# Row sums of three norms: one product of plain float32 with ones replaced by two products of rounded parts

## The chip, the cores and the metric

The kernel runs on one core of a Trainium2 chip. The metric is the device time of one execution in microseconds. Three executions of the kernel before took 1333.63 to 1334.12 us, with a median of 1333.63 us.

## The reference

Two transformer blocks in float32, applied one after the other to 512 tokens of width 1024. The first has four mixers (short convolution, stick-breaking attention, a Mamba-2 mixer, block attention), gates, an output projection and a gated feed-forward net of hidden width 2816. The second has sliding-window attention with sinks, spatial gating and an output projection. The change concerns the places where a row's mean square is taken:

```python
def rmsnorm(x, g):
    xf = x.astype(jnp.float32)
    y = xf * lax.rsqrt(jnp.mean(xf * xf, axis=-1, keepdims=True) + RMS_EPS)
    return (y * g.astype(jnp.float32)).astype(x.dtype)
...
    x = x + merged @ w_o
    h2 = rmsnorm(x, norm2_g)                      # norm 1 of the change
    g_ff, up_ff = jnp.split(h2 @ w_gate_up, 2, axis=-1)
    return x + (jax.nn.silu(g_ff) * up_ff) @ w_down
...
    return rmsnorm(h, final_g)[:, :seq]           # norm 2: end of the first block
...
        h = rmsnorm_2(x, norm_g[l])               # norm 3: start of the second block
        proj = h @ w_in[l]
```

## The kernel before

Activations lie with features on the 128 partitions and the 512 tokens along a row: `xT` is eight tiles of 128x512. Every weight matrix is streamed in **units** of 1024 (or fewer) rows by 256 columns; a unit gives two output **tiles** of 128x512, in one of four PSUM banks `G` each. All large products are made in three parts of a rounded type (fp32r): a weight is split into `whi` (rounded, a copy by ScalarE, `split(n)`) and `wlo` (the rest, four subtractions of 128x512 by GpSimd), an activation into `hh` and `hl`. One tile of a unit is `gemm_fm`: eight times `whi` with `hh` and with `hl` (lines 592 and 593), then eight times `wlo` with `hh` (line 600). `unit_last_k` does the same for the first unit behind a norm, but leaves the three products of the last k for both tiles to the end (lines 659 to 661), since that piece of `hh` and `hl` comes last.

Each engine has a program of its own, in an order written out by hand, and they are tied by semaphores. An engine carries out its program in order: behind an instruction that waits, all later ones of its engine wait. `hi_done` counts the finished `whi` (a unit's first product waits for its own), `lo_done` the finished halves of `wlo`, `tile_done` and `tile_free` the PSUM tiles.

A norm is not applied ahead of its product. The weights are multiplied with `x*g`, and the result is scaled with `R`, the reciprocal root of the row's mean square, spread over the partitions. For `R` the squares of the eight tiles are added on VectorE into `acc0` (128x512), and TensorE multiplies that with a 128x128 matrix of ones (`ones`, in the constants `c1`), which sums over the partitions and spreads the sum: line 893. ScalarE takes the root from the bank `M[0]` (lines 1142 and 1143). For the two norms between the blocks there are `acc1` and `acc2` (lines 909 and 910), and `R` is made from both in a longer chain between ScalarE and VectorE. These products are plain float32.

What ScalarE has to do behind these sums, in its order:

```python
            act.wait_ge(sem("norm_ps"), 1)
            rsqrt(R[:, :], M[0][:, :], DM).then_inc(sem("R2"), 1)

            for f, (n0, part, h0) in enumerate(ffn_units):
                with act.Fori(0, part // 2) as i:
                    for j in range(2):
                        n = n0 + j
                        split(n + 1, i)
```

So `whi` of the second feed-forward unit is made behind the wait for the first sum (`norm_ps` 1). Behind the second sums (`norm_ps` 2) stand, in this order, lines 1347, 1348, 1350, 1142 and 1143 (the roots), the wait for `key_s` (VectorE makes it from `R`), four DMA issues of `key_t` (line 1360), and then `split` of the unit `n_qz + 1`.

The names of the units around the two places: `n_c0` to `n_c0 + 3` are the output projection of block one; the feed-forward units begin at `ffn_units[0]` (below "the first feed-forward unit"); `n_e0` is the unit of keys and values of block two, `n_qz` and `n_qz + 1` are the first of its queries and gates. `turn_rows` and `turn_keys` are small transposes (lines 917, 922 and 930) that stand between tiles of `n_qz`; `turn_rows` needs `R` of the second block (semaphore `R3`).

Of the kernel before, what the change touches and what calls it, by code (L numbers as in the profile page):

```python
# [27 lines left out]
SEQ, DM = 512, 1024  # L28
P = 128
KD = DM // P  # L30
# [45 lines left out]
def build_program(nc, x, par, cst1, cst2a, w_in, w_branch, w_o, w_gu, w_down, w_in2, sg_w, sg_b, ln_g,  # L76
                  ln_b, w_ao, w_so, w_o2, out):
    f32, f32r = mybir.dt.float32, mybir.dt.float32r
# [6 lines left out]
    with ctx:  # L85
        base = (nc.sbuf_base + 31) // 32 * 32

        def place(name, shape, kb, dt=f32):

            return nc.alloc_sbuf_tensor_at(name, shape, dt, offset=base + int(kb * KB))  # L90
# [3 lines left out]
        def sem(name):  # L94
            if name not in sems:
                sems[name] = ctx.enter_context(nc.semaphore(name))
            return sems[name]
# [10 lines left out]
        hh = place("hh", [P, KD, SEQ], 76, f32r)  # L108
        hl = place("hl", [P, KD, SEQ], 92, f32r)
        c1 = place("c1", [P, 640], 108)  # L110
        prm = place("prm", [P, NPAR], 112)
        sml = place("sml", [P, 256], 113)
        R = place("R", [P, SEQ], 114)
        Z0 = 116.0
# [42 lines left out]

        acc0 = place("acc0", [P, SEQ], Z0)
        sq0 = place("sq0", [P, 2, SEQ], Z0 + 2)

        ah = place("ah", [P, 8, SEQ], Z0, f32r)
        al = place("al", [P, 8, SEQ], Z0 + 16, f32r)
# [1 line left out]
        fu_t = place("fu_t", [P, 2, SEQ], Z0 + 68)  # L164
        acc1 = place("acc1", [P, SEQ], Z0 + 32)
        acc2 = place("acc2", [P, SEQ], Z0 + 34)
        sq1 = place("sq1", [P, 2, SEQ], Z0 + 36)
        sq2 = place("sq2", [P, 2, SEQ], Z0 + 40)
        r1 = place("r1", [P, SEQ], Z0 + 44)
# [112 lines left out]
        def as_f32(ap):  # L282
            return ap.bitcast(f32)
# [288 lines left out]
        def _(pe):  # L572
# [64 lines left out]
            def unit_last_k(n, xh, xl, kts, ready, between=None, between_at=0):  # L637

                last_k, s = kts - 1, n % 2
                tiles = [(bank_of(tiles_before(n) + j), j * P) for j in range(2)]  # L640
                for j, (bank, col) in enumerate(tiles):
                    pe.wait_ge(sem("tile_free"), free_before(tiles_before(n) + j))
                    if j == 0:
                        pe.wait_ge(sem("hi_done"), n + 1)
                    for k in range(last_k):
                        if j == 0:
                            pe.wait_ge(sem(ready[0]), ready[1] + k + 1)
                        w = whi[:, s, k, col:col + P]
                        mm(bank[:, :], w, xh[:, k, :], start=(k == 0), stop=False)  # L649
                        mm(bank[:, :], w, xl[:, k, :], start=False, stop=False)  # L650
                    pe.wait_ge(sem("lo_done"), 2 * n + 1 + j)
                    for k in range(last_k):
                        mm(bank[:, :], wlo[:, s, k, col:col + P], xh[:, k, :], start=False, stop=False)  # L653
                    if between and j == between_at:
                        between()
                pe.wait_ge(sem(ready[0]), ready[1] + kts)
                for bank, col in tiles:
                    w = whi[:, s, last_k, col:col + P]
                    mm(bank[:, :], w, xh[:, last_k, :], start=False, stop=False)
                    mm(bank[:, :], w, xl[:, last_k, :], start=False, stop=False)  # L660
                    mm(bank[:, :], wlo[:, s, last_k, col:col + P], xh[:, last_k, :], start=False, stop=True).then_inc(sem("tile_done"), 1)
# [227 lines left out]
            for f, (n0, part, h0) in enumerate(ffn_units):  # L889
                if f == 0:  # L890
                    def sum_rows():
                        pe.wait_ge(sem("acc0"), KD)
                        mm(M[0][:, :], ones, acc0[:, :], start=True, stop=True).then_inc(sem("norm_ps"), 1)
                    unit_last_k(n0, hh, hl, KD, ("h_lo", KD), sum_rows)
                    unit_fm(n0 + 1)
                with pe.Fori(1 if f == 0 else 0, part // 2) as i:
                    for s in range(2):
                        n = 2 * i + n0 + s
                        for j in range(2):
                            b = (tiles_before(n0) + 2 * s + j) % 4  # L900
                            gemm_fm((4 * i + tiles_before(n0) + 2 * s + j, b), n, (n0 + s) % 2, hh, hl, KD, j * P, j == 0)
                unit_last_k(n0 + part, ah, al, part, ("act_lo", h0))
                for p in range(1, 4):
                    unit_fm(n0 + part + p, ah, al, part)


            def sum_both():
                pe.wait_ge(sem("acc2"), KD)
                mm(M[0][:, :], ones, acc1[:, :], start=True, stop=True)
                mm(M[1][:, :], ones, acc2[:, :], start=True, stop=True).then_inc(sem("norm_ps"), 1)  # L910
            unit_last_k(n_e0, hh, hl, KD, ("h_lo", 2 * KD), sum_both, 1)

            def turn_rows():

# [81 lines left out]
            for p in range(4):  # L996
                n = n_qz + 2 * p
                for u in range(2):
                    for j in range(2):
                        gemm_fm(tiles_before(n + u) + j, n + u, (n + u) % 2, hh, hl, KD, j * P, j == 0,  # L1000
                                hooks={at: w_slot for at in W_AT[2 * u + j]} if p else None)
                        if p == 0 and u == 0:
                            (turn_rows, turn_keys)[j]()
            for p in range(4):
                n = n_vs + p
                wide_unit(n, p % 2, tiles_before(n - p % 2), lambda t: w_slot())
# [514 lines left out]
        def _(dve):  # L1521
# [4 lines left out]
            def link(ins):  # L1526

                links[0] += 1
                ins.then_inc(sem("dve_link"), 1)
                dve.wait_ge(sem("dve_link"), links[0])  # L1530
# [35 lines left out]

            dve.wait_ge(sem("r_ps"), 1)
            link(v.tensor_copy(R[:, :], M[0][:, :]))
            v.memset(cbuf[:, :, 0:2], 0.0)
            link(v.memset(xbuf[:, :, 0:3], 0.0))  # L1570
            link(v.memset(wdt[:, :, :], 0.0))
# [248 lines left out]
            def accumulate(acc, sq, m, name):  # L1820
                if m == 0:
                    v.tensor_copy(acc[:, :], sq[:, 0, :]).then_inc(sem(name), 1)
                else:
                    dve.wait_ge(sem(name), m)
                    tt(acc[:, :], acc[:, :], sq[:, m % 2, :], ALU.add).then_inc(sem(name), 1)
# [5 lines left out]
            for m in range(KD):  # L1831
                add_residual(tiles_before(n_c0) + m, m)
                dve.wait_ge(sem("h_hi"), KD + m + 1)
                stt(out=hl[:, m, :], in0=xT[:, m, :], scalar=pcol("g2", m), in1=as_f32(hh[:, m, :]),
                    op0=ALU.mult, op1=ALU.subtract).then_inc(sem("h_lo"), 1)
                dve.wait_ge(sem("sq0"), m + 1)
                accumulate(acc0, sq0, m, "acc0")
            dve.wait_ge(sem("R2"), 1)


# [39 lines left out]


            dve.wait_ge(sem("acc1"), KD)
            v.memset(key_t[:, :, :], 0.0)
            link(v.memset(rope_t[:, :, :], 0.0))
            dve.wait_ge(sem("rms12"), 1)
# [321 lines left out]
```

## Time and profile before

| what | value |
|---|---|
| median of three executions | 1333.63 us |
| the profiled execution | 1333.23 us |
| its span, first to last instruction | 1331.2 us |
| TensorE busy | 1321.4 us, 99% of the span |
| VectorE, ScalarE, GpSimd busy | 582.5, 509.6, 597.1 us (44, 38, 45%) |
| mean granted TensorE clock | 0.998 of full speed |
| share of DMA queue q1 of its engines' span | 30.7% |

What lies outside the span is 2.0 us. A row of the timeline gives the start in us, the duration in us, the engine (PE is TensorE, DVE is VectorE, ACT is ScalarE, POOL is GpSimd), the line, the instruction, what it writes and reads, the shape and how many are taken together; in brackets stands how long the engine was idle before and what released it. TensorE's products are pipelined: one of 128x512 is shown as 0.39 us long, while the next starts before it has ended, so the cost of one is the distance of starts. A plain float32 product appears as two records.

### The profile page before, as it was taken

How to read it: one execution, taken by the hardware profiler on the slowest of the kernel's cores; microseconds unless marked ns; L12 is line 12 of the kernel's file. 1: busy time of each engine (PE TensorE's matmuls, PEld its weight loads, DVE VectorE, ACT ScalarE, POOL GpSimd, SP SyncE). 2: the span in 40 equal slices, each digit the busy share in tenths (PEclk: the TensorE clock that was granted, in tenths of full speed). 3: DMA queues.
4: the chain of work that ended last, by engine and by line, in shares of the span. 5: the costliest groups of instructions: out<-in, count | busy, mean ns of one | idle time of the engine just before them, and what ended most of it. 6: DMA issues, size and time to landing. Idle time of an engine off the chain costs nothing.

```text
span 1331.2 us, 16999 instructions
## 1 busy us (share of the span) xinstructions
PE 1321.4 (99%) x6518; PEld 1081.4 (81%) x6518; DVE 582.5 (44%) x947; ACT 509.6 (38%) x729; POOL 597.1 (45%) x448
## 2 busy tenths in 40 slices
PE   9999999999999999999999999999999999999998
PEld 8877777888888888888888887877777888888887
DVE  3674444556554433213322347766654322242333
ACT  6222534566433533222211236254655224342233
POOL 4453333443644364445554546433432553435441
PEclk9999999999999999999999999999999999999999
DMA  6333152413233343333333323322221332423321
GB/s 202 95 113 102 40 151 64 126 41 119 79 97 134 95 115 106 95 95 95 95 95 95 87 71 111 103 69 77 91 68 59 127 95 64 127 64 100 102 83 64
DMA packets 144493, 126.70 MB, mean 95 GB/s; under 512 B 4464, under 2 KB 139760, under 8 KB 144432
## 3 DMA queue, kind: packets, MB, share of 16 engines
q1 hardware_dynamic: 144080, 125.66, 30.7%
q8 instruction: 43, 0.70, 0.2%
q10 hardware_dynamic: 352, 0.19, 0.1%
q14 instruction: 18, 0.15, 0.0%
HBM read 120.46 MB, written 2.10 MB: 92 GB/s over the span
## 4 chain that ended last, share of the span: by engine, by line
PE 96%; DVE 2%; ACT 1%; issue 0%; DMA 0%; SPq 0%; ACTq 0%; DVEq 0%
PE gemm L592 25%; PE gemm L600 25%; PE gemm L593 25%; PE gemm L649 2%; PE gemm L650 2%; PE gemm L653 2%; PE gemm L616 2%; PE gemm L617 2%; PE gemm L622 2%; PE mix L978 1%; PE mix L966 1%; PE mix L955 1%; PE mix L1032 1%; PE mix L802 1%; PE gemm L677 1%; PE mix L827 0%
## 5 line engine op out<-in xcount | busy, mean ns | idle before, releaser
L525 POOL TENSOR_TENSOR wlo<-raw,whi 128x512 fp32r<-128x512 f32 x424 | 571.9, 1379 | 551.0 <-ACT whi L1130 551.0
L592 PE MATMUL gemm<-hh,whi 128*128 128x512 f32 x1128 | 444.9, 394 | 0.4 <-ACT whi L1130 0.4
L593 PE MATMUL gemm<-hl,whi 128*128 128x512 f32 x1128 | 439.6, 390 | 0.0
L600 PE MATMUL gemm<-hh,wlo 128*128 128x512 f32 x1128 | 280.3, 390 | 0.0
L1130 ACT ACTIVATE whi<-raw 128x2048 fp32r<-128x2048 f32 x106 | 202.5, 1911 | 193.4 <-PE gemm L600 164.6
L592 PEld LDWEIGHTS gemm<-hh,whi 128*128 128x128 f32 x1128 | 211.8, 188 | 49.2 <-issue 4.6
L593 PEld LDWEIGHTS gemm<-hl,whi 128*128 128x128 f32 x1128 | 212.0, 188 | 43.1 <-issue 0.5
L600 PEld LDWEIGHTS gemm<-hh,wlo 128*128 128x128 f32 x1128 | 211.4, 188 | 43.6
L521 POOL TENSOR_TENSOR wlo_b<-raw_b,whi_b 128x512 fp32r<-128x512 f32 x16 | 20.6, 1287 | 146.2 <-ACT whi L1130 146.2
L1850 DVE TENSOR_TENSOR fu_t<-gemm,R 128x512 f32<-128x512 f32 x22 | 15.2, 691 | 99.7 <-PE gemm L600 99.7
L592 PE MATMUL gemm<-ah,whi 128*128 128x512 f32 x132 | 51.5, 390 | 0.5 <-DVE xT L1829 0.5
L593 PE MATMUL gemm<-al,whi 128*128 128x512 f32 x132 | 51.4, 389 | 0.0
L1797 DVE TENSOR_TENSOR gt<-gemm,R 128x512 f32<-128x512 f32 x32 | 22.0, 688 | 65.5 <-PE gemm L600 65.4
L1147 ACT ACTIVATE gt<-gt 128x512 f32<-128x512 f32 x32 | 20.1, 627 | 71.7 <-DVE gt L1797 71.7
L1327 ACT ACTIVATE fg_t<-fg_t 128x512 f32<-128x512 f32 x22 | 13.9, 633 | 84.6 <-DVE fg_t L1848 84.6
L1869 DVE TENSOR_TENSOR xT<-xT,gemm 128x512 f32 x16 | 11.0, 687 | 70.0 <-PE gemm L600 57.0
L616 PE MATMUL gemm<-whi,hh 128*128 128x512 f32 x96 | 39.2, 408 | 0.0
L617 PE MATMUL gemm<-whi,hl 128*128 128x512 f32 x96 | 37.6, 391 | 0.0
L1848 DVE TENSOR_TENSOR fg_t<-gemm,R 128x512 f32<-128x512 f32 x22 | 15.2, 691 | 48.1 <-PE gemm L600 39.8
L1857 DVE TENSOR_TENSOR al<-fu_t,ah 128x512 f32 x22 | 34.7, 1576 | 2.7
L600 PE MATMUL gemm<-ah,wlo 128*128 128x512 f32 x132 | 33.0, 390 | 0.0
L1371 ACT ACTIVATE wp<-mix,sml 128x256 f32<-128x256 f32 (+1 forms) x64 | 27.7, 452 | 10.5 <-DVE sml L1947 10.5
(443 smaller groups left out, 1863.9 us busy)
## 6 DMA issues: line engine op xcount, KB each, us to landing
raw<-w_in SPq DMA_DIRECT2D x53, 1024.0 KB, 5.3
raw<-w_gu SPq DMA_DIRECT2D x44, 512.0 KB, 4.7
raw<-w_o SPq DMA_DIRECT2D x8, 1024.0 KB, 5.1
raw<-w_down SPq DMA_DIRECT2D x16, 512.0 KB, 4.0
raw_b<-w_branch SPq DMA_DIRECT2D x16, 256.0 KB, 5.6
raw<-w_ao SPq DMA_DIRECT2D x4, 1024.0 KB, 5.1
raw<-w_so SPq DMA_DIRECT2D x4, 1024.0 KB, 5.0
raw<-w_in SPq DMA_DIRECT2D x7, 512.0 KB, 4.6
```

The source lines that it names most:

```text
L525: last = nc.gpsimd.tensor_tensor(a(wlo), a(raw), as_f32(a(whi)), ALU.subtract)
L592: mm(bank[:, :], w, xh[:, k, :], start=(k == 0), stop=False)
L593: mm(bank[:, :], w, xl[:, k, :], start=False, stop=False)
L600: last = mm(bank[:, :], wlo_[:, s, k, col:col + P], xh[:, k, :], start=False, stop=(k == kts - 1))
L616: mm(o, hh[:, 4 * half + i, tok], w, start=(half == 0 and i == 0), stop=False)
L617: mm(o, hl[:, 4 * half + i, tok], w, start=False, stop=False)
L622: last = mm(o, hh[:, 4 * half + i, tok], w, start=False, stop=(half == 1 and i == 3))
L649: mm(bank[:, :], w, xh[:, k, :], start=(k == 0), stop=False)
L650: mm(bank[:, :], w, xl[:, k, :], start=False, stop=False)
L1130: fn(a(whi), a(raw), ACT.Copy).then_inc(sem("hi_done"), 1)
L1371: last = fn(wp[:, s % 3, h, w_from(s):], w_score[:, h, e, w_from(s):], ACT.Exp, bias=w_min(v)[:, h, e:e + 1], accum_out=w_sums(v)[:, h, e, ...
L1857: tt(flat(al), fu_t[:, s, :], as_f32(flat(ah)), ALU.subtract).then_inc(sem("act_lo"), 1)
```

## The change

For each of the three sums VectorE splits the accumulated squares into a rounded part (`acc0h`, `acch`) and a rest (`acc0l`, `accl`), both in the rounded type, and TensorE multiplies each with a rounded matrix of ones (`ones_r`, copied once at the start) and adds the two in PSUM. The first sum moves from behind the first tile of its unit to behind the second. The two later sums move out of unit `n_e0` into the first tile of `n_qz`, behind its tenth product; `turn_rows` moves from between the tiles of `n_qz` to behind the tenth product of the second tile.

```diff
@@ [buffers]
+        ones_r = place("ones_r", [P, P], 110.5, f32r)
...
+        acc0h = place("acc0h", [P, SEQ], Z0 + 6, f32r)
+        acc0l = place("acc0l", [P, SEQ], Z0 + 8, f32r)
...
+        acch = place("acch", [P, 2, SEQ], Z0 + 48, f32r)
+        accl = place("accl", [P, 2, SEQ], Z0 + 52, f32r)
@@ [TensorE]
                     def sum_rows():
-                        pe.wait_ge(sem("acc0"), KD)
-                        mm(M[0][:, :], ones, acc0[:, :], start=True, stop=True).then_inc(sem("norm_ps"), 1)
-                    unit_last_k(n0, hh, hl, KD, ("h_lo", KD), sum_rows)
+                        pe.wait_ge(sem("ones_r"), 1)
+                        pe.wait_ge(sem("acc0_lo"), 2)
+                        mm(M[0][:, :], ones_r[:, :], acc0h[:, :], start=True, stop=False)
+                        mm(M[0][:, :], ones_r[:, :], acc0l[:, :], start=False, stop=True).then_inc(sem("norm_ps"), 1)
+                    unit_last_k(n0, hh, hl, KD, ("h_lo", KD), sum_rows, 1)
...
             def sum_both():
-                pe.wait_ge(sem("acc2"), KD)
-                mm(M[0][:, :], ones, acc1[:, :], start=True, stop=True)
-                mm(M[1][:, :], ones, acc2[:, :], start=True, stop=True).then_inc(sem("norm_ps"), 1)
-            unit_last_k(n_e0, hh, hl, KD, ("h_lo", 2 * KD), sum_both, 1)
+                pe.wait_ge(sem("acc_lo"), 3)
+                for i in range(2):
+                    mm(M[i][:, :], ones_r[:, :], acch[:, i, :], start=True, stop=False)
+                    last = mm(M[i][:, :], ones_r[:, :], accl[:, i, :], start=False, stop=True)
+                last.then_inc(sem("norm_ps"), 1)
+            unit_last_k(n_e0, hh, hl, KD, ("h_lo", 2 * KD))
...
                         gemm_fm(tiles_before(n + u) + j, n + u, (n + u) % 2, hh, hl, KD, j * P, j == 0,
-                                hooks={at: w_slot for at in W_AT[2 * u + j]} if p else None)
-                        if p == 0 and u == 0:
-                            (turn_rows, turn_keys)[j]()
+                                hooks={at: w_slot for at in W_AT[2 * u + j]} if p else {10: (sum_both, turn_rows)[j]} if u == 0 else None)
+                        if p == 0 and u == 0 and j == 1:
+                            turn_keys()
@@ [VectorE]
             link(v.tensor_copy(R[:, :], M[0][:, :]))
+            dve.wait_ge(sem("c1_in"), 16)
+            v.tensor_copy(ones_r[:, :], ones).then_inc(sem("ones_r"), 1)
...
                 accumulate(acc0, sq0, m, "acc0")
+            dve.wait_ge(sem("acc0"), KD)
+            v.tensor_copy(acc0h[:, :], acc0[:, :]).then_inc(sem("acc0_lo"), 1)
+            dve.wait_ge(sem("acc0_lo"), 1)
+            tt(acc0l[:, :], acc0[:, :], as_f32(acc0h[:, :]), ALU.subtract).then_inc(sem("acc0_lo"), 1)
             dve.wait_ge(sem("R2"), 1)
...
             dve.wait_ge(sem("acc1"), KD)
+            v.tensor_copy(acch[:, 0, :], acc1[:, :])
+            dve.wait_ge(sem("acc2"), KD)
+            v.tensor_copy(acch[:, 1, :], acc2[:, :]).then_inc(sem("acc_lo"), 1)
+            dve.wait_ge(sem("acc_lo"), 1)
+            for i, a in enumerate((acc1, acc2)):
+                tt(accl[:, i, :], a[:, :], as_f32(acch[:, i, :]), ALU.subtract).then_inc(sem("acc_lo"), 1)
             v.memset(key_t[:, :, :], 0.0)
```

ScalarE's and GpSimd's programs have the same instructions in the same order as before. What moves is shown for TensorE at the two places. (`mix` is a bank of `M`, `gemm` one of `G`, `c_58` holds `ones` and the identity.)

**The first feed-forward unit.** Before, the sum stands between its two tiles:

```order
L653 MATMUL gemm<-hh,wlo 128x512 [waits lo_done]
L653 MATMUL gemm<-hh,wlo 128x512 x6
L893 MATMUL mix<-acc_103,c_58 128x512 [waits acc0]
L649 MATMUL gemm<-hh,whi 128x512 [waits tile_free]
L650 MATMUL gemm<-hl,whi 128x512
```

Now the second tile's 21 products come first, then the two products of the sum, the six of the last k, and the first of the next unit:

```order
L658 MATMUL gemm<-hh,wlo 128x512 [waits lo_done]
L658 MATMUL gemm<-hh,wlo 128x512 x6
L899 MATMUL mix<-acc0h,ones_r 128x512 [waits acc0_lo,ones_r]
L900 MATMUL mix<-acc0l,ones_r 128x512
L664 MATMUL gemm<-hh,whi 128x512 [waits h_lo]
...
L597 MATMUL gemm<-hh,whi 128x512 [waits hi_done,tile_free]
```

The sum moved behind 21 products; behind its own two products only six more lie ahead of the next unit's wait for `hi_done`.

**Between the blocks.** Before, the two sums stand ahead of the last six products of `n_e0`:

```order
L653 MATMUL gemm<-hh,wlo 128x512 x6
L909 MATMUL mix<-acc_109,c_58 128x512 [waits acc2]
L910 MATMUL mix<-acc_110,c_58 128x512
L659 MATMUL gemm<-hh,whi 128x512 [waits h_lo]
...
L592 MATMUL gemm<-hh,whi 128x512 [waits hi_done,tile_free]
```

Now they stand in the first tile of `n_qz`, and `turn_rows` (lines 926 and 931) in the second:

```order
L597 MATMUL gemm<-hh,whi 128x512 [waits hi_done,tile_free]
...
L917 MATMUL mix<-acch,ones_r 128x512 [waits acc_lo]
L918 MATMUL mix<-accl,ones_r 128x512
L917 MATMUL mix<-acch,ones_r 128x512
L918 MATMUL mix<-accl,ones_r 128x512
...
L926 MATMUL mix<-c_58,R 128x128 [waits R3]
L926 MATMUL mix<-c_58,R 128x128 x3
L931 MATMUL mix<-c_58,sgw 128x128 [waits sgw_in]
L931 MATMUL mix<-c_58,sgw 128x128 x7
```

The sums moved behind 16 products (six of `n_e0`, ten of `n_qz`).

ScalarE's rows behind the second sums are the same in both kernels but for line numbers; here they are of the changed one:

```order
L1356 ACTIVATE r_118<-mix,prm 128x512 [waits norm_ps]
L1357 ACTIVATE r_119<-r_118 128x512 [waits act_link]
L1359 ACTIVATE r_118<-r_118 128x512 [waits rms12]
L1151 ACTIVATE r_119<-r_119,prm 128x512 [waits n3_var]
L1152 ACTIVATE r_119<-r_119 128x512 [waits act_link]
L1363 ACT_TABLE_LOAD
L1369 DMA key_t<-key_s 8x512 [waits key_s]
L1369 DMA key_t<-key_s 8x512 x3
L1139 ACTIVATE whi<-raw 128x2048 [waits tile_done,raw_in0]
```

The last row is the split of `n_qz + 1`; nothing moved here.

## Rows read from the trace of the kernel before

**Rows 1.** Clock of the core, and the chain that ended last, by engine

```profile
core 0: 1331.2 us, clock 0.998
PE 96%; DVE 2%; ACT 1%; issue 0%; DMA 0%; SPq 0%; ACTq 0%; DVEq 0%
```

**Rows 2.** Timeline, TensorE, first feed-forward unit and the start of the next

```profile
459.05 1.02 PE L893 MATMUL mix<-acc,c 128*128 128x512 f32 x2
...
464.72 0.39 PE L659 MATMUL gemm<-hh,whi 128*128 128x512 f32 x1
...
466.08 0.39 PE L592 MATMUL gemm<-hh,whi 128*128 128x512 f32 x1
```

**Rows 3.** Timeline, ScalarE, same stretch

```profile
460.11 0.69 ACT L1142 ACTIVATE R<-mix,prm 128x512 f32<-128x512 f32 x1 [2.35 <-PE mix L893]
...
462.77 1.92 ACT L1130 ACTIVATE whi<-raw 128x2048 fp32r<-128x2048 f32 x1
```

**Rows 4.** Timeline, VectorE and GpSimd, same stretch

```profile
456.64 0.68 DVE L1825 TENSOR_TENSOR acc<-acc,sq 128x512 f32<-128x512 f32 x1
...
464.77 11.13 POOL L525 TENSOR_TENSOR wlo<-raw,whi 128x512 fp32r<-128x512 f32 x8 [11.81 <-ACT whi L1130]
```

**Rows 5.** Timeline, TensorE, units n_e0, n_qz, first product of n_qz + 1

```profile
825.90 1.02 PE L909 MATMUL mix<-acc,c 128*128 128x512 f32 x2
...
827.84 0.40 PE L660 MATMUL gemm<-hl,whi 128*128 128x512 f32 x1
...
829.00 0.40 PE L592 MATMUL gemm<-hh,whi 128*128 128x512 f32 x1
...
834.47 0.60 PE L917 MATMUL mix<-c,R 128*128 128x128 f32 x4
...
835.69 0.47 PE L592 MATMUL gemm<-hh,whi 128*128 128x512 f32 x1
...
841.62 0.48 PE L592 MATMUL gemm<-hh,whi 128*128 128x512 f32 x1
```

**Rows 6.** Timeline, ScalarE, behind the second sums (ACTq: DMA issues)

```profile
827.81 0.69 ACT L1347 ACTIVATE r<-mix,prm 128x512 f32<-128x512 f32 x1 [0.71 <-PE mix L910]
...
834.29 3.70 ACTq L1360 DMA_DIRECT2D key_t<-key_s  x4
838.10 1.92 ACT L1130 ACTIVATE whi<-raw 128x2048 fp32r<-128x2048 f32 x1 [5.42 <-issue]
```

**Rows 7.** Timeline, VectorE and GpSimd, around the second sums

```profile
824.02 1.29 DVE L1825 TENSOR_TENSOR acc<-acc,sq 128x512 f32<-128x512 f32 x2 [0.38 <-ACT sq L1342]
...
831.41 0.69 DVE L1888 TENSOR_TENSOR R<-r,r 128x512 f32<-128x512 f32 x1 [1.46 <-ACT r L1143]
...
825.87 5.01 POOL L525 TENSOR_TENSOR wlo<-raw,whi 128x512 fp32r<-128x512 f32 x4 [3.22 <-ACT whi L1130]
```

**Rows 8.** Timeline, VectorE and GpSimd, copies and subtractions beside each other

```profile
489.70 0.43 DVE L1855 TENSOR_SCALAR ah<-fu_t 128x512 f32 x1
490.25 1.62 DVE L1857 TENSOR_TENSOR al<-fu_t,ah 128x512 f32 x1
...
490.03 5.49 POOL L525 TENSOR_TENSOR wlo<-raw,whi 128x512 fp32r<-128x512 f32 x4 [5.09 <-ACT whi L1130]
...
468.03 1.28 DVE L1855 TENSOR_SCALAR ah<-fu_t 128x512 f32 x1 [0.16 <-DVE fu_t L1853]
...
818.23 3.27 DVE L1825 TENSOR_TENSOR acc<-acc,sq 128x512 f32<-128x512 f32 x2
```

**Rows 9.** Timeline, TensorE, a short wait for whi

```profile
1027.83 0.50 PE L592 MATMUL gemm<-hh,whi 128*128 128x512 f32 x1 [0.42 <-ACT whi L1130]
```

**Rows 10.** Timeline, TensorE, start of the program

```profile
1.06 4.21 PE L677 MATMUL gemm<-warm 128*128 128x128 f32 x18 [1.06 <-DVE warm L1554]
...
6.21 2.62 PE L677 MATMUL gemm<-warm 128*128 128x128 f32 x22
```

## The prediction

> **What bounds the kernel now.** I read the chain that ended last first: 96% of it is TensorE, at a mean granted clock of 0.998, its upper level of 2.4 GHz [rows 1]. So TensorE's own work and its pauses are the time, and whatever else lies beside it costs nothing until TensorE waits for it. Then I read the timeline of TensorE at the three sums, for what a product costs and where the next wait for another engine stands; then ScalarE's timeline at the same places, for what is queued behind the sum; then VectorE and GpSimd.
>
> A product of the rounded type costs 0.227 us: the six of the last k run from 464.72 to 466.08 [rows 2]. Below that is a slot. Two plain float32 sums cost 827.84 - 825.90 less one slot, 1.71 us, so 0.86 each [rows 5].
>
> **What the change takes away.** Three products of 0.86 become six slots. 2.57 - 1.36 = 1.2 us less for TensorE: 0.4 at the first place, 0.8 at the second. That is 0.09% of the time, under half of the 0.2% that a measurement of this kernel can tell from no change.
>
> **What VectorE gets.** One copy of 128x128 at the start, far smaller than the 128x512 copy beside which I price it: at most the 0.43 us of `ah` [rows 8]. VectorE goes into the next tiles with TensorE tens of slots away from needing them, and the constants it waits for have already served the transposes that released it. I count nothing, at worst 0.4 for the queue behind it on VectorE, which TensorE would not feel. Then three casts and three subtractions of 128x512. No cast from float32 to the rounded type stands on VectorE before. The nearest row is `ah`, one input, one output of the same shape: 0.43 us, or 1.28 with GpSimd busy [rows 8]. The subtraction is like `al`.
>
> At the first place this is free. The last addition ends at 456.64 + 0.68 = 457.32 [rows 4]. Cast and subtraction, 1.28 + 1.62 at their worst, are done by 460.3 with handovers, and GpSimd sleeps until 464.77 [rows 4], so rather by 458.7. TensorE comes for them at 463.8 (below).
>
> **First place, the sum that comes later.** This decides. The sum is not on ScalarE's way by accident: behind its wait stand the two root instructions, a table load, and `whi` of the next unit, and TensorE starts that unit with a wait for this `whi`. Before, ScalarE starts at 460.11, which is 0.04 after the sum's last record ends (459.05 + 1.02 = 460.07), and `whi` runs from 462.77 to 464.69 [rows 2, 3]. TensorE starts the unit at 466.08 [rows 2]. So there are 1.4 us to spare.
>
> After: the second tile starts at 459.05, where the sum stood. 21 slots take 4.76, so the sum starts at 463.81, its second product at 464.04, and that record ends 0.39 later, at 464.43. ScalarE starts at 464.47, 4.36 later than before. Nothing behind it gets shorter, so `whi` runs from 467.13 to 469.05. TensorE ends the sum at 464.27 and the six last products at 465.63, and waits 3.4 us. The handover takes 0.08 or less (`whi` ends at 464.69, GpSimd starts at 464.77 [rows 3, 4]); the first product after such a pause is 0.50 long, not 0.39 [rows 9], 0.11 more. TensorE is where it was at 466.08 at about 469.2. **Place one: +3.1 us**, the gain of 0.4 already in it.
>
> Is something else late next? GpSimd needs 1.39 a subtraction (11.13 for eight [rows 4]); the first half of `wlo` is there 2.9 after `whi`, at 472.0. TensorE wants it after 16 slots, at 472.8. It holds, with 0.8 to spare. The unit after that has the whole 10.9 us of a unit for its `whi`.
>
> **Second place.** Without the sums the six last products run from 825.90 to 827.26, and `n_qz` starts there instead of at 829.00. Its `whi` is ready, since GpSimd began on it at 825.87 [rows 5, 7]. Ten slots later, at 829.53, TensorE wants the four split tiles.
>
> VectorE's last addition ends at 824.02 + 1.29 = 825.31 [rows 7]. Two casts of 0.43 bring it to 826.1 or 826.2. From 825.87 GpSimd works beside it. A subtraction that met GpSimd just after it had begun ended 1.84 after GpSimd's start (490.25 + 1.62 - 490.03 [rows 8]). Two such one behind the other, from 826.0 on, end at 829.7. TensorE waits 0.2 for them and starts the sums at 829.73. The lower end: two additions beside GpSimd took 3.27 together [rows 8], so 829.45, no wait. The upper end: one cast also meets GpSimd and takes 1.28, which moves everything by 0.85 to 1.0: a wait of 1.2. I take 0.2, as the single row describes this case, a start right behind GpSimd's.
>
> On this the Trainium skill, "SBUF — State Buffer", section "Who interferes with whom", says that one pair of ports serves both engines, that a VectorE instruction with two SBUF inputs collides with a GpSimd one that reads SBUF, and that who comes second is blocked for the other's whole instruction. By that rule each subtraction waits out one of GpSimd's 1.25 us (5.01 / 4) and then takes 0.69, and the two end at 829.9; by the row of the two additions it is 829.45. The sum would be larger by 0.2 or smaller by 0.2.
>
> Now ScalarE. Before it starts at 827.81 [rows 6], again 0.04 behind the last record (827.18 + 0.59). After: the fourth product starts at 829.73 + 0.68, ends at 830.80, ScalarE starts at 830.84: 3.03 later. The whole chain behind it hangs together: roots, `R` at 831.41 on VectorE [rows 7], `key_s`, four DMA issues from 834.29 for 3.70, then `whi` of `n_qz + 1` from 838.10 to 840.02 [rows 6]. All of it moves by 3.03, so that `whi` is ready at 843.05. Before, TensorE needed it at 841.62 [rows 5], 1.6 after it was ready.
>
> What does TensorE do until then? From 829.73 four slots and 14 slots end the first tile at 833.8. Ten slots more bring it to `turn_rows` at 836.1. That needs `R`, 832.10 + 3.03 = 835.13: no wait. The transposes take 1.22 (834.47 to 835.69 [rows 5]), 14 slots end the tile at 840.5, `turn_keys` takes under 0.4. TensorE stands at `n_qz + 1` at 840.9 and starts at 843.1, a wait of 2.2. Against 841.62: **place two: +1.5 us**. The slow first product was there before too (0.48 [rows 5]), so no extra for it. The queries' DMAs on SP and GpSimd's subtractions, which hang on the same chain, come 3.0 later as well, but the units behind need them some 10 us on.
>
> **Sum.** 3.1 + 1.5 = +4.6 us on the profiled execution's 1333.23, so 1337.8. The median shown is 0.4 above that execution, so I predict 1338.2, 0.34% slower. Should ends be taken at their lower bounds it is 1337.4, with the late casts 1339.3: that is the main case's own range.
>
> **Rivals.**
>
> *The clock falls in the first pause.* For it: 3.4 us without a product is three times the longest wait that TensorE has anywhere now, the 1.06 at the start [rows 10]. The first 18 records of the program took 4.21 us, 0.234 each, the next 22 only 0.119 each [rows 10], which is what 1.2 and 2.4 GHz would give. A second start like that loses 4.21 - 18 x 0.119 = 2.1 us: 1340.3. Against it: the array worked without a gap up to the pause, and before the start it had not worked at all. The Trainium skill, "TensorE: Matmul & The Clock Gate", section "HAM oscillation — how this bites in real kernels", says that a long enough pause puts the array back to half clock and that the next work then begins cold; no trace here shows a pause of this length. Chance 0.13.
>
> *The casts are slow or collide.* One more microsecond at place two, 1339.2. For it: the one 1.28 in rows 8; against: the casts come before GpSimd starts. Chance 0.14.
>
> *The pauses at place two are swallowed.* If the chain behind the second sums is shorter than it seems, or its DMA issues were waiting for something that doesn't move, only the gain of 0.8 is left there: 3.1 - 0.8, 1335.9, within 0.2% of now. Against it: the rows join without a gap. Chance 0.07. If place one is swallowed instead: -0.4 + 1.5, 1334.7. Chance 0.04.
>
> *No wait at all: not slower.* If the `whi` at 462.77 belonged to a unit that TensorE needs one unit later, there would be 10.9 us more to spare, both delays would vanish, and what stays is the 1.2 of the products: 1332.4, no measurable change. It decides at a delay of 1.4 us at place one (I have 4.36) and 1.6 at place two (3.03). Against it: the order of ScalarE's program names the unit, and GpSimd begins 0.08 after it. Chance 0.08.
>
> *A later wait grows from these.* `wlo` late at place one by more than its 0.8 to spare, or the attention's first steps: 1341 or more. Chance 0.04.
>
> **The numbers.** The main case has 0.50. Slower by over 0.2% (above 1336.3): 0.50 + 0.13 + 0.14 + 0.04 = 0.81. Within 0.2%: 0.07 + 0.04 + 0.06 of the 0.08. Faster by over 0.2% needs 2.7 us where all the sums together cost 2.6: only the remaining 0.02. The range reaches down to the case of one swallowed place and up to the fallen clock: 1335.8 to 1340.4.
>
> **What would show it.** The sums: six records of 0.39 a slot apart, none of 0.59. First place: ScalarE's root 4.4 after where it was in relation to the unit's start, `whi` 4.4 later, and a wait of TensorE for `whi` of 3.4 us, by far the longest of the run. Second place: a wait of 0 to 0.3 at the sums for VectorE, one of about 2 at `n_qz + 1` for `whi`. If the granted clock dips after the first wait, the second rival holds. If TensorE shows no wait for `whi` at either place, I have read ScalarE's order wrongly, and the time will be under the one before.

## The result, and the profile after

The changed kernel takes 1339.99 us, the median of six executions (1338.94 to 1340.73). Six of the kernel before beside it took 1333.60 us (1333.50 to 1334.12). The ratio is 1.0046, with an interval of 1.0036 to 1.0057: slower by 6.4 us, where 4.6 were forecast.

The profiled execution took 1339.9 us, 6.67 more than the one of before. Its span and clock, the chain that ended last, and TensorE's waits:

```profile
core 0: 1337.8 us, clock 0.997
```

```profile
PE 95%; DVE 2%; ACT 2%; DMA 1%; issue 0%; ACTq 0%; SPq 0%; DVEq 0%
```

```profile
PE gemm L597 <- ACT whi L1139: 5.5, 3, 3.4
PE gemm L682 <- DVE warm L1563: 1.1, 1, 1.1
...
PE mix L674 <- DMA xtm<-x: 0.6, 1, 0.6
```

The first row has grown: 5.5 us in three waits for a `whi`, the longest of them 3.4, where the kernel before has one such wait, of 0.4 us. The chain is still TensorE's, so what counts is where its timeline is longer than before. First the first feed-forward unit, which answers to [rows 2]:

```profile
464.37 0.39 PE L899 MATMUL mix<-acc0h,ones_r 128*128 128x512 f32 x1
464.60 0.39 PE L900 MATMUL mix<-acc0l,ones_r 128*128 128x512 f32 x1
...
465.96 0.39 PE L666 MATMUL gemm<-hh,wlo 128*128 128x512 f32 x1
469.75 0.77 PE L597 MATMUL gemm<-hh,whi 128*128 128x512 f32 x1 [3.40 <-ACT whi L1139]
470.31 0.63 PE L598 MATMUL gemm<-hl,whi 128*128 128x512 f32 x1
```

The two products of the sum stand one slot apart and cost a slot each. Then come the six of the last k, and then 3.40 us of nothing. ScalarE's rows say what it was doing, as in [rows 3]:

```profile
465.03 0.69 ACT L1151 ACTIVATE R<-mix,prm 128x512 f32<-128x512 f32 x1 [6.70 <-PE mix L900]
...
467.69 1.91 ACT L1139 ACTIVATE whi<-raw 128x2048 fp32r<-128x2048 f32 x1
```

It stood idle for 6.70 us at the wait for the sum, with the split of the next unit queued behind. Behind the pause the products are 0.77 and 0.63 long instead of 0.39. Two stretches of windows there (length; busy time of PE, PEld, DVE, ACT, POOL; granted clock; DMA share; GB/s):

```profile
469.70:472.70 3.00, 2.96 (x7) 2.41 (x8) 1.12 (x1) 2.99 (x3) 3.00 (x3) 0.50 0.00 0
473.10:476.50 3.40, 3.40 (x16) 2.80 (x15) 2.65 (x2) 0.24 (x1) 3.40 (x3) 1.00 0.01 3
```

The granted clock is 0.50 for the first three microseconds, which is 1.2 GHz, with 7 products begun in them; then it is full again. It had fallen at 469.4, while TensorE still stood idle. Between the blocks, answering to [rows 5]:

```profile
831.16 0.39 PE L664 MATMUL gemm<-hh,whi 128*128 128x512 f32 x1
...
834.78 0.42 PE L917 MATMUL mix<-acch,ones_r 128*128 128x512 f32 x1
...
841.18 0.60 PE L926 MATMUL mix<-c,R 128*128 128x128 f32 x4
...
845.96 0.63 PE L939 MATMUL mix<-c,wpt 128*128 128x128 f32 x4
848.28 0.47 PE L597 MATMUL gemm<-hh,whi 128*128 128x512 f32 x1 [1.69 <-ACT whi L1139]
```

and the rows of ScalarE that answer to [rows 6]:

```profile
835.93 0.69 ACT L1356 ACTIVATE r<-mix,prm 128x512 f32<-128x512 f32 x1 [3.60 <-PE mix L918]
...
842.42 3.71 ACTq L1369 DMA_DIRECT2D key_t<-key_s  x4
846.23 1.91 ACT L1139 ACTIVATE whi<-raw 128x2048 fp32r<-128x2048 f32 x1 [5.42 <-PE gemm L605]
```

**The account.** Three marks on TensorE's timeline stand at the same work in every version. S is the first product behind the first tile of the first feed-forward unit, before or after that the sum. U is the first product of the next unit. V is the first product behind the second tile's `wlo` products of `n_e0`, or where TensorE comes to it if it has to wait there. W is the first product of `n_qz + 1`.

| stretch | before | after | difference |
|---|---|---|---|
| start to S | 459.05 | 459.61 | +0.56 |
| S to U, place one | 7.03 | 10.14 | +3.11 |
| U to V | 359.82 | 361.41 | +1.59 |
| V to W, place two | 15.72 | 17.12 | +1.40 |

The sum is 6.66 of 6.67. The 1.59 lie in a stretch in which the change touches nothing, and the time at half clock accounts for them: TensorE works from 469.75 to about 472.8 at 0.50, and half of that is 1.5. The 0.56 begin with the 0.6 us wait for the first piece of `x` in the list of waits.

### The profile page after: what moved, and what is told of

The parts are those of the page before. It is cut to its first block, busy times and chain, and to the rows that moved or that the text cites. A ratio compares the mean times of both kernels' runs of the same rounds, so it can differ in the third digit from the quotient of the medians.

```text
span 1337.8 us, 17008 instructions
## 1 busy us (share of the span) xinstructions
PE 1322.3 (99%) x6518; PEld 1081.9 (81%) x6518; DVE 590.9 (44%) x954; ACT 509.7 (38%) x729; POOL 598.1 (45%) x448
## 4 chain that ended last, share of the span: by engine, by line
PE 95%; DVE 2%; ACT 2%; DMA 1%; issue 0%; ACTq 0%; SPq 0%; DVEq 0%
PE gemm L597 25%; PE gemm L598 25%; PE gemm L605 25%; PE gemm L654 2%; PE gemm L655 2%; PE gemm L658 2%; PE gemm L621 2%; PE gemm L622 2%; PE gemm L627 2%; PE mix L987 1%; PE mix L975 1%; PE mix L964 1%; PE mix L1041 1%; PE mix L807 1%; PE mix L832 0%; PE mix L790 0%
```

## The experiments

Each was timed in five rounds beside the kernel before, whose median was 1333.46 us (27 executions) for the first four, 1333.29 (22) for the next four, and 1333.40 (21) for the last two. Edits are against the changed kernel unless said otherwise. None leaves out work. The theory: ScalarE's wait for a sum holds up the `whi` behind it, at both places, and the first pause drops the clock. The rivals: the rounded products or the splits cost the time, or the move of the first sum matters by something else than what ScalarE has queued.

**1. `sum1_back`: the first sum back in its old place, still rounded.**

```diff
-                    unit_last_k(n0, hh, hl, KD, ("h_lo", KD), sum_rows, 1)
+                    unit_last_k(n0, hh, hl, KD, ("h_lo", KD), sum_rows)
```

> The changed kernel with its first sum back between the two tiles of the first feed-forward unit (both products still of rounded parts). Times against 1333.6 us of the kernel before. Theory A (the loss is ScalarE's whi of the next unit queued behind the later sum, plus half clock after that pause): the pause of 3.4 us and the half clock of 1.5 us go, 0.4 us is gained there, place two still costs 1.4 us, so +1.0 us, about 1334.6. Theory B (the loss comes with the split itself: VectorE's casts and subtractions, their collisions with GpSimd, the copy at the start, the buffers): nothing of that goes, only the 3.1 us of the measured pause, or less, so above 1336.

1334.14 us (1333.76 to 1336.66, 11 executions), ratio 1.0007, interval 0.9998 to 1.0016. Almost all of the loss is gone with one argument, so at place one it is no cost of the rounded form. Place two is as in the changed kernel, 17.14 from V to W:

```profile
842.43 0.47 PE L597 MATMUL gemm<-hh,whi 128*128 128x512 f32 x1 [1.68 <-ACT whi L1139]
```

One of the eleven took 1336.66; no trace shows why.

**2. `place2_undone`: the second sums and `turn_rows` as before, the first as changed.**

```diff
...
+                pe.wait_ge(sem("acc2"), KD)
+                mm(M[0][:, :], ones, acc1[:, :], start=True, stop=True)
+                mm(M[1][:, :], ones, acc2[:, :], start=True, stop=True).then_inc(sem("norm_ps"), 1)
-            unit_last_k(n_e0, hh, hl, KD, ("h_lo", 2 * KD))
+            unit_last_k(n_e0, hh, hl, KD, ("h_lo", 2 * KD), sum_both, 1)
...
```

(The hooks in `n_qz` and VectorE's casts and subtractions there go too.)

> The changed kernel with everything between the blocks as before (plain float32 sums in unit n_e0, transposes between the tiles of n_qz, no casts); place one as changed. Theory A: 3.1 us of place one and 1.5 us of half clock, +4.6, about 1338.2. Theory B: the three of six VectorE instructions that collide with GpSimd stand at place two, so most of the loss beyond the 3.1 us goes and it is near 1336.7.

1338.54 us (1337.74 to 1338.79), ratio 1.0037, interval 1.0024 to 1.0051. That is 1.45 below the changed kernel, which is place two's share (1.40 in the table). Here too the first pause costs the clock: U to V is 361.49.

```profile
469.10 0.77 PE L597 MATMUL gemm<-hh,whi 128*128 128x512 f32 x1 [3.40 <-ACT whi L1137]
```

**3. `whi1_first`: the sum stays late, but ScalarE makes the next unit's `whi` ahead of its wait for it.**

```diff
+            split(n_d0 + 1)
             act.wait_ge(sem("norm_ps"), 1)
```

(`n_d0` is the first feed-forward unit; the loop behind then leaves this one split out.)

> The changed kernel with ScalarE's whi of the second feed-forward unit ahead of its wait for the first sum (the first pass of its loop is written out). The sum stays late. Theory A: TensorE no longer waits there, and its clock stays at the upper level: -0.4 + 1.4 = +1.0 us, about 1334.6, the same as with the sum moved back. If the later sum itself hurts (R too late for VectorE and the PSUM tiles), a pause of another kind stays and it is above 1336.

1333.70 us (1333.40 to 1334.62), ratio 1.0002, interval 0.9993 to 1.0011. This tells the theory from "the sum is bad there": TensorE's program is the changed one, and only what is queued behind ScalarE's wait differs. The profiled execution took 1334.62, as expected, with the stretches of `sum1_back` at both places (6.57 and 17.14); the median is 0.9 lower, and no trace of a faster execution shows why.

```profile
465.79 0.39 PE L666 MATMUL gemm<-hh,wlo 128*128 128x512 f32 x1
466.02 0.39 PE L597 MATMUL gemm<-hh,whi 128*128 128x512 f32 x1
```

No pause; S to U is 6.57, which is 0.46 less than before: the time that the rounded sum saves. U to V is 359.83, so the 1.59 went with the pause.

**4. `whi_both_first`: `whi1_first`, and the same at place two, ahead of ScalarE's wait for the second sums.**

```diff
+            split(n_qz + 1)
             act.wait_ge(sem("norm_ps"), 2)
```

(This comes on top of the edit of `whi1_first`; the loop behind leaves this split out too.)

> As the last, and whi of n_qz + 1 also ahead of ScalarE's wait for the second sums. Theory A: both pauses go and what the change takes from TensorE's products is seen: -1.2 us, with up to 0.3 us for the transposes of the keys that then wait for VectorE, so 1332.4 to 1332.8, faster than the kernel before. Theory B: above 1334.

1334.51 us (1333.86 to 1334.79), ratio 1.0008, interval 0.9999 to 1.0017. This missed: the wait for `whi` is gone, and the time is 1.7 above the upper end of what I expected, in the range that I had given to the rival. The trace doesn't bear that rival out at place one (S to U is 6.57, U to V 359.82). At place two V to W is 17.22, no less than in the changed kernel, since TensorE waits elsewhere:

```profile
842.30 0.64 PE L939 MATMUL mix<-c,wpt 128*128 128x128 f32 x4 [1.78 <-DVE sml L1940]
```

The transposes of the keys are late, since VectorE is. VectorE and GpSimd there:

```profile
825.47 11.38 POOL L530 TENSOR_TENSOR wlo<-raw,whi 128x512 fp32r<-128x512 f32 x8 [3.22 <-ACT whi L1139]
...
833.90 1.82 DVE L1918 TENSOR_TENSOR R<-r,r 128x512 f32<-128x512 f32 x1 [1.46 <-ACT r L1152]
...
835.85 2.15 DVE L1926 TENSOR_TENSOR cs<-cs,R 128x512 f32<-128x512 f32 x2
```

With `whi` early, GpSimd goes through eight subtractions without a break, 825.47 to 836.85, and VectorE's short chain `R` and `cs`, which the keys need, runs beside it: `R` takes 1.82 us, not 0.69, and the two multiplications for `cs` 2.15, where they take 1.29 in `whi2_between` below.

**5. `late_sum_only`: the kernel before, with nothing but the first sum's move, in plain float32.** (Edit against the kernel before.)

```diff
-                    unit_last_k(n0, hh, hl, KD, ("h_lo", KD), sum_rows)
+                    unit_last_k(n0, hh, hl, KD, ("h_lo", KD), sum_rows, 1)
```

> The kernel before with one edit: its first sum, plain float32 as it was, moved behind the second tile. No rounded parts anywhere. Theory A (position and ScalarE's order are all of place one): ScalarE starts 4.8 us later, TensorE waits until 469.5 instead of starting at 466.1, +3.5 us, and half clock behind that costs 1.5 us: +5.0, about 1338.6. Theory B (the rounded parts cost it): no change, 1333.6, or at most the 3.5.

1339.12 us (1338.39 to 1339.54), ratio 1.0040, interval 1.0027 to 1.0054. The move alone makes the loss of place one, without a rounded product in the kernel: S to U is 10.54, 3.51 more than before, where 3.5 were expected. The clock fell again, and for longer:

```profile
469.48 0.76 PE L592 MATMUL gemm<-hh,whi 128*128 128x512 f32 x1 [3.36 <-ACT whi L1130]
```

```profile
468.00:469.00 1.00, 0.00 (x0) 0.00 (x0) 0.00 (x0) 1.00 (x1) 0.00 (x0) 0.77 0.00 0
...
470.00:475.20 5.20, 5.20 (x14) 4.00 (x13) 3.61 (x3) 3.06 (x3) 5.20 (x5) 0.50 0.00 0
...
475.00:475.50 0.50, 0.50 (x3) 0.36 (x2) 0.50 (x1) 0.00 (x0) 0.50 (x2) 0.62 0.00 0
```

The means of the first and the last of these rows put the fall at about 468.5, in the pause, and the rise at about 475.4: 6.8 us at 0.50, of which TensorE works 5.9. Half of 5.9 is 2.95, and U to V is 362.69, 2.87 more than before. The start of this kernel also waits for `x`, without a copy of `ones_r` in it, so such a wait needs nothing of the change:

```profile
5.17 1.06 PE L669 MATMUL mix<-c,xtm 128*128 128x128 f32 x8 [0.29 <-DMA xtm<-x]
```

**6. `pause_filled`: the changed kernel with 14 products in the first pause, into a bank that nobody reads.**

```diff
+                    for _ in range(14):
+                        mm(M[1][:, :], ones_r[:, :], hh[:, 0, :], start=True, stop=True)
```

> The changed kernel with 14 products of 128x512 into a PSUM bank that nothing reads, put where TensorE waits at place one (3.2 of the 3.4 us). They add work but only in the pause. If the half clock follows from the pause, it stays at the upper level: 3.1 + 1.4 = +4.5 us, about 1338.1, 1.5 us faster than the changed kernel, and with little spread from run to run. If the clock falls for another reason (the sums, their operands), it falls here too and the time stays at about 1340.

1337.68 us (1337.46 to 1337.97), ratio 1.0031, interval 1.0019 to 1.0044. The delay is untouched, the emptiness is gone:

```profile
465.34 3.33 PE L903 MATMUL mix<-hh,ones_r 128*128 128x512 f32 x14
468.91 0.47 PE L597 MATMUL gemm<-hh,whi 128*128 128x512 f32 x1 [0.23 <-ACT whi L1141]
```

```profile
468.90:472.30 3.40, 3.39 (x15) 2.81 (x16) 1.40 (x2) 3.39 (x3) 3.40 (x3) 1.00 0.00 0
```

S to U is 10.14, as in the changed kernel; the clock stays at 1.00, and U to V is 359.97 instead of 361.41. This shows that the 1.4 to 1.6 us behind the pause are the clock's, and that idleness brings them, not the lateness of `whi`. The median is 2.3 below the changed kernel's, more than the 1.44 of this stretch. In the profiled executions, 2.2 apart, S at 458.77 instead of 459.61 makes the rest; of the medians' difference 0.3 lies between the kernels before that were timed beside the two (1333.60 and 1333.29).

**7. `rounded_sums_old_place`: rounded form everywhere, no sum moved.** (`sum1_back`, and `sum_both` and `turn_rows` in their old places.)

```diff
...
-            unit_last_k(n_e0, hh, hl, KD, ("h_lo", 2 * KD))
+            unit_last_k(n_e0, hh, hl, KD, ("h_lo", 2 * KD), sum_both, 1)
...
```

> Rounded parts everywhere, but every sum at its old place: the first between the tiles, the later two ahead of the last six products of n_e0. Place one: -0.4 us. Place two: TensorE comes for the split tiles at 825.9 and they are done 4.1 us after the last addition, at 829.4, so it waits 3.5 us; the sums are 0.8 us shorter; the rest of ScalarE's chain moves by as much as TensorE: +2.7 us. Theory A on the clock (a pause of this length lets it fall whatever the cause): 1.5 us more, +3.8 in all, about 1337.4. If only a wait for ScalarE did that: +2.3, 1335.9.

1337.22 us (1335.24 to 1339.51, 11 executions), ratio 1.0029, interval 1.0020 to 1.0038. At the old place the split tiles are not ready, and TensorE waits for VectorE:

```profile
828.79 0.50 PE L917 MATMUL mix<-acch,ones_r 128*128 128x512 f32 x1 [3.32 <-DVE accl L1903]
```

```profile
830.40:833.70 3.30, 3.30 (x10) 2.53 (x9) 1.26 (x3) 3.02 (x6) 0.73 (x1) 0.50 0.00 0
```

So at place two the rounded form needs the move: V to W is 20.09 here, counted from 825.32, where TensorE comes to the sums, and 17.12 with the move. Some 1.7 of the 20.09 is the clock's (half of the 3.4 us at 0.50), which leaves 1.3 for the place alone. This pause, for another engine and at another place, was followed by half clock too, though only 1.5 us behind its end.

**8. `half_pause`: the first sum ahead of the second tile's `wlo` products, half way.**

```diff
+                    if between and between_at == 1.5 and j == 1:
+                        between()
...
-                    unit_last_k(n0, hh, hl, KD, ("h_lo", KD), sum_rows, 1)
+                    unit_last_k(n0, hh, hl, KD, ("h_lo", KD), sum_rows, 1.5)
```

> The changed kernel with its first sum seven products earlier, ahead of the wlo products of the second tile, so that TensorE's wait for whi is 1.8 us instead of 3.4. If the shorter pause leaves the clock alone: 3.1 - 1.6 + 1.4 = +2.9 us, about 1336.5. If any pause of this size lets it fall: +4.4, about 1338.

1337.18 us (1335.62 to 1338.66, 11 executions), ratio 1.0026, interval 1.0017 to 1.0036. S to U is 8.55. The pauses at the two places are as long as each other:

```profile
468.31 0.47 PE L597 MATMUL gemm<-hh,whi 128*128 128x512 f32 x1 [1.81 <-ACT whi L1141]
...
845.48 0.47 PE L597 MATMUL gemm<-hh,whi 128*128 128x512 f32 x1 [1.77 <-ACT whi L1141]
```

```profile
846.50:849.80 3.30, 3.30 (x9) 2.62 (x8) 3.11 (x7) 1.66 (x1) 3.30 (x4) 0.50 0.45 118
```

The clock did not fall behind the first and did behind the second, 1 us later. In the changed kernel a second pause of 1.69 left it alone. So a pause of this length can cost the clock and need not; what decides, these traces don't show. The eleven times lie in clusters some 1.5 us apart (four from 1335.6 to 1336.4, four from 1337.2 to 1337.4, three from 1338.3 to 1338.7), which would fit zero, one and two falls; but the one trace lies in the last cluster and shows one fall, beside a start 0.7 us later than the kernel before has it, so this reading isn't shown.

**9. `whi2_between`: first sum back, and at place two the split of `n_qz + 1` behind ScalarE's two roots and its table load, ahead of its wait for `key_s`.**

```diff
+            split(n_qz + 1)
             act.wait_ge(sem("key_s"), 1)
```

(and the loop behind leaves it out)

> The first sum back between its tiles, and ScalarE's whi of n_qz + 1 between the roots and the wait for key_s, not ahead of the roots. With whi ahead of the roots TensorE no longer waited for it, but 1.8 us for the transposes of the keys: GpSimd's subtractions then lay over VectorE's making of R and its use (those instructions took 1.1 and 0.9 us more). Theory: that collision ate the gain. Here GpSimd starts only when VectorE has begun on key_s, whose instructions have one input in PSUM. Expected: -0.4 at place one, -0.8 at place two, up to 0.2 for the transposes of the keys: 1332.3 to 1332.6, a span of 1330.0 to 1330.4 if the start costs nothing extra, and no wait of TensorE over 0.5 us between the blocks. If the collision was not the cause, the wait of 1.8 us stays and the time is 1334 or above.

1332.15 us (1331.86 to 1333.15, 11 executions), against 1333.40: 1.25 below. The ratio of 0.9993 has an interval of 0.9984 to 1.0002, so it is not certain to be faster than the kernel before; its median is the lowest of all that ran. The profiled executions are 0.98 apart, which is 0.46 at place one and 0.52 at place two.

```profile
840.22 0.63 PE L939 MATMUL mix<-c,wpt 128*128 128x128 f32 x4
840.61 0.48 PE L597 MATMUL gemm<-hh,whi 128*128 128x512 f32 x1
```

```profile
833.80 0.69 DVE L1910 TENSOR_TENSOR R<-r,r 128x512 f32<-128x512 f32 x1 [1.46 <-ACT r L1152]
...
837.08 5.05 POOL L530 TENSOR_TENSOR wlo<-raw,whi 128x512 fp32r<-128x512 f32 x4 [5.76 <-ACT whi L1139]
...
839.99 0.15 DVE L1932 COPY sml<-mix 128x4 f32<-128x4 f32 x1
```

No wait for `whi` is left. It runs from 835.08 to 837.00, while VectorE makes `cs` and `key_s`; GpSimd starts at 837.08, behind both and not over them, and `R` takes 0.69 again. V to W is 15.20, 0.52 less than before. The missing 0.3 of the 0.8 that two rounded sums save stands at `turn_keys`: it begins 0.08 behind the end of VectorE's copy `sml` (840.14), and 2.08 behind the start of the eight `wlo` products ahead of it, where eight slots are 1.82. This is the place at which `whi_both_first` waited 1.78.

**10. `first_sum_alone`: `sum1_back` and `place2_undone` together.** Only the first sum is rounded, in its old place.

> The least of the change: only the first sum of rounded parts, at its old place, and everything between the blocks as before. Expected: 0.4 us less than before, 1333.1, which the interval will not tell from no change; in the trace the unit behind the first sum starts 7.2 us after the sum does at 6.6. If the cast and subtraction come late, TensorE shows a wait for VectorE at the sum instead.

1332.77 us (1332.46 to 1333.60, 11 executions), ratio 0.9997, interval 0.9988 to 1.0006. The expectation compares 7.2 and 6.6 for the stretch from S to U; the old one is 7.03, and here it is 6.57:

```profile
458.97 0.39 PE L899 MATMUL mix<-acc0h,ones_r 128*128 128x512 f32 x1
...
465.54 0.39 PE L597 MATMUL gemm<-hh,whi 128*128 128x512 f32 x1
```

TensorE doesn't wait for VectorE: the split tiles of the first sum are ready even at the old place. Its gain never needed the move.

## Why the prediction was right in its range and wrong in its main case

The measured 1339.99 lies in the stated range (1335.8 to 1340.4), but not by the main case, whose 1338.2 is 1.8 too low and whose own range ended at 1339.3. It lies there because the range reached up to a rival that I gave a chance of 0.13, and that rival, priced at 1340.3, came true. The direction and both waits for `whi` came as forecast; that the whole came within the range is in part luck.

**The step that failed** is the choice of the main case, which left the clock out: "The clock falls in the first pause", chance 0.13. (The prediction's last paragraph calls it the second rival; it is the first in the list.) It fell in the changed kernel and in the two versions that kept its 3.4 us pause empty (`place2_undone`, `late_sum_only`); where the pause was filled, or gone, it did not fall at place one. The argument against, "the array worked without a gap up to the pause", gave no protection: TensorE was busy with hardly a break for 460 us before. The rival had the mechanism right and the price near: 2.1 us, from the slow first records at the start [rows 10], where 1.59 was measured, 361.41 less 359.82, with TensorE working some 3.1 us at half clock. The Trainium skill, "TensorE: Matmul & The Clock Gate", section "HAM oscillation — how this bites in real kernels", says that a long enough pause puts the array back to half clock; the window at 0.50 behind the 3.40 agrees. I put that behind an argument that no row supported.

**Place one, +3.1:** measured 3.11 from S to U. The terms hold one by one. The sum was to start 4.76 behind the second tile's start (464.37 - 459.61 = 4.76); ScalarE's root at 465.03, 0.04 behind the second record's end (464.60 + 0.39); the pause 3.4 us (3.40). `whi1_first` shows that this is the queue behind ScalarE's wait and nothing of the sum's own.

**Place two, +1.5:** measured 1.40, from terms that were each a little off. For the rows here take off 5.26, the distance of the two kernels at V (831.16 - 825.90).

The wait for the split tiles was forecast at 0.2, and the sum started within 0.01 of its slot: 834.78, sixteen slots behind 831.16. VectorE's rows answer to [rows 7]:

```profile
830.46 0.42 DVE L1898 CAST acch<-acc 128x512 fp32r<-128x512 f32 x1
830.80 0.42 DVE L1900 CAST acch<-acc 128x512 fp32r<-128x512 f32 x1
831.25 3.39 DVE L1903 TENSOR_TENSOR accl<-acc,acch 128x512 fp32r<-128x512 f32 x2
```

The casts cost what `ah` did [rows 8], 0.42 against 0.43. The subtractions began at 825.99, as the forecast's 826.0 has it, though the prediction let the casts end at 826.1 or 826.2; the second cast started 0.34 behind the first and not 0.43. The two subtractions took 3.39 us together and ended at 834.64 - 5.26 = 829.38, not 829.7: the row of two additions (829.45) described them, the single row (two in sequence of 1.84 each) did not. The Trainium skill's rule, "SBUF — State Buffer", section "Who interferes with whom", gave 829.9; by the measured end it was the furthest off, so here two subtractions beside GpSimd do better than waiting out one of its instructions each. GpSimd paid too: its four subtractions there took 5.94 us, where they took 5.01 before [rows 7].

ScalarE's chain came 835.93 - 5.26 - 827.81 = 2.86 later, not 3.03, and everything behind it moved along: `whi` ended at 848.14 - 5.26 = 842.88, forecast 843.05. TensorE's wait came out shorter, since it got there later and the profile counts from a record's end. `turn_keys` starts at 845.96, and where nothing is waited for the next product starts 0.39 behind that (840.61 - 840.22 in `whi2_between`); so TensorE stood there at 846.35 - 5.26 = 841.09, where 840.9 was forecast. The 0.2 are a small wait that I missed, for VectorE's `sml`, which hangs on the same chain. None of it changes when `n_qz + 1` starts, and that counts.

**The sums:** each rounded product stands one slot from the next, as forecast. At place one 0.46 came out as time where 0.4 was forecast (`whi1_first`), at place two 0.52 of the 0.8 (`whi2_between`). The 0.3 missing at place two are the wait for `sml`. **Start:** the copy to `ones_r` costs TensorE nothing that a trace shows. The 0.56 before S are a difference between executions: S lies between 458.77 and 459.76 in the traces of all the versions, the earliest is that of `pause_filled`, which has the copy, and `late_sum_only`, without it, waits for `x` as well.

**Sum:** 3.11 + 1.40 = 4.5 for what was forecast as 4.6, then 1.6 for the clock, which in medians gives 1333.6 + 6.1 = 1339.7 against 1339.99. The lower end of the main case's own range, 1337.4, is not worked out in the prediction; the one term that it names there, no wait at the sums, gives 1338.0.

**What stays open:** why the half clock lasted 6.8 us in `late_sum_only` and 3.4 in the others, and why pauses of 1.7 to 1.8 us cost the clock in one place and not in another. That `rounded_sums_old_place` and `half_pause` spread over 3 to 4 us where `pause_filled` keeps within 0.5 fits with falls that come in some executions only, at pauses of 3.3 us too (three of eleven executions of `rounded_sums_old_place` took 1335.2 to 1335.4, 1.7 below the traced one), but I have one trace of each version.

## What to carry to other kernels

Before moving a product later, read what the engine that waits for it has queued behind that wait, and which of it TensorE needs first: here the moved product had 1.4 us to spare and was moved by 4.4, and to save 0.4 it cost 3.1, the saving taken off. Price a new pause of TensorE twice, by its length and by the clock behind it. If the work queued behind the wait is moved ahead of it, look where the next engine's work then falls: `whi` ahead of the roots pushed GpSimd over VectorE's chain and gave back what it won; `whi` behind them did not.

## What the runs showed of the hardware

- Every empty pause of 3.3 to 3.4 us (four traces) came with a stretch at a granted clock of 0.50, 3.4 us long in three and 6.8 in one; it cost 1.6 and 1.7 us (U to V of the changed kernel and of `place2_undone`) and 2.9 in the long one, about half of the time that TensorE worked at 0.50 in each (3.1, 3.3 and 5.9 us). Behind the three waits for `whi` of 3.4 us TensorE's first product already ran at the low clock (0.77 and 0.76 us long, where it is 0.47 at full clock); in `rounded_sums_old_place` the fall came 1.5 us after TensorE had gone on.
- One pause of 1.77 us was followed by it too, 1.0 us after its end; six others of 1.68 to 1.81 were not.
- Fourteen products with a result that nobody reads, over 3.33 us, kept the clock up.
- Beside GpSimd's subtractions a VectorE multiplication of 128x512 took 1.82 instead of 0.69 us (`whi_both_first`); with GpSimd's work some microseconds later it took 0.69 (`whi2_between`). It goes both ways: four GpSimd subtractions beside two of VectorE took 5.94 instead of 5.01 (changed kernel).
